# A two-layer decoder trunk in split fp32 on one core: another order for its opening (whole rows of x, products k-tile by k-tile, the first norm from x's rows, low parts shared with GpSimd)

## The reference

```
h = h + 0.5 * RMSNorm_post(SwiGLU(RMSNorm_pre(h)))            # ffn1: d_ff = 2816
h = h + RMSNorm_post(W_out [pool | conv | GLA](RMSNorm_pre(h) @ W_in))
h = h + 0.5 * RMSNorm_post(SwiGLU(RMSNorm_pre(h)))            # ffn2
swiglu(h) = (silu(h @ wg) * (h @ wu)) @ wd
rms_norm(x, g) = x * rsqrt(mean(x*x, -1) + 1e-6) * g
```

## Time and profile before

| | |
|---|---|
| median of 3 runs | 1019.27 us (1018.76, 1019.27, 1021.01) |
| span of the profiled execution | 1017.5 us; the median of the runs is 1.8 us above it, which stands for what lies around the span, as this execution's own time outside the profiler is not listed |
| PE busy | 99% |
| DVE, ACT, POOL busy | 60%, 49%, 25% |
| first matmul on weights | 9.77 us after the span's start |
| first matmul of unit 2 | 25.08 us |

### The profile page before, as it was taken

How to read it: one execution, slowest core, us unless ns; L and a number is a source line. 1 busy time by engine, 2 the same in 40 slices (tenths; PEclk the granted TensorE clock), 3 DMA queues, 4 the chain that set the end, 5 groups by cost and what they waited for, 6 DMA issues and landing times.

```text
span 1017.5 us, 21484 instructions
## 1 busy us (share of the span) xinstructions
PE 1008.4 (99%) x9002; PEld 985.1 (97%) x9002; DVE 614.5 (60%) x610; ACT 498.4 (49%) x565; POOL 256.0 (25%) x179
## 2 busy tenths in 40 slices
PE   8999999999999999999999999999999999999997
PEld 8999999999999999999999999999999999999886
DVE  5744554588968744554477445544889687554452
ACT  5544343566556544443555443435665665434331
POOL 0333330112402333330103333301124014333200
PEclk9999999999999999999999999999999999999999
DMA  9865536635345665435747653357353547666621
GB/s 295 256 202 167 160 114 197 223 125 166 127 141 173 216 192 176 129 114 184 231 131 224 192 166 129 114 194 225 125 167 126 168 149 249 186 191 200 197 73 42
DMA packets 164197, 173.88 MB, mean 171 GB/s; under 512 B 9372, under 2 KB 150936, under 8 KB 164136
## 3 DMA queue, kind: packets, MB, share of 16 engines
q1 hardware_dynamic: 161960, 171.01, 52.9%
q10 hardware_dynamic: 2176, 1.98, 0.8%
HBM read 171.91 MB, written 1.06 MB: 170 GB/s over the span
## 4 chain that ended last, share of the span: by engine, by line
PE 97%; ACT 1%; DMA 1%; DVE 1%; SPq 0%; issue 0%; DVEq 0%
PE ps L1408 25%; PE ps L1410 25%; PE ps L1409 25%; PE ps L1440 2%; PE ps L1425 2%; PE ps L1441 2%; PE ps L1636 2%; PE ps L1635 2%; PE ps L1637 2%; PE ps L1559 2%; PE ps L1600 2%; PE ps L1601 2%; PE ps L1783 1%; DMA raw<-in_ffn_wu 1%; PE ps L1467 1%; ACT w_hi L555 0%
## 5 line engine op out<-in xcount | busy, mean ns | idle before, releaser
L848 DVE TENSOR_TENSOR w_lo<-raw,w_hi 128x2048 fp32r<-128x2048 f32 (+2 forms) x174 | 382.8, 2205 | 278.1 <-ACT w_hi L555 277.7
L1408 PE MATMUL ps<-x_hi,w_hi 128*128 128x272 f32 (+2 forms) x1608 | 462.4, 288 | 0.5 <-DVE w_lo L1026 0.5
L1410 PE MATMUL ps<-x_hi,w_lo 128*128 128x272 f32 (+2 forms) x1608 | 460.3, 286 | 0.0
L1409 PE MATMUL ps<-x_lo,w_hi 128*128 128x272 f32 (+2 forms) x1584 | 453.2, 286 | 0.0
L555 ACT ACTIVATE w_hi<-raw 128x2048 fp32r<-128x2048 f32 (+3 forms) x175 | 312.8, 1791 | 203.1 <-PE ps L1410 142.9
L1408 PEld LDWEIGHTS ps<-x_hi,w_hi 128*128 128x128 f32 x1608 | 302.8, 188 | 2.2 <-DVE w_lo L1026 0.7
L1410 PEld LDWEIGHTS ps<-x_hi,w_lo 128*128 128x128 f32 x1608 | 302.3, 188 | 0.0
L1409 PEld LDWEIGHTS ps<-x_lo,w_hi 128*128 128x128 f32 x1584 | 298.2, 188 | 0.1
L1326 POOL TENSOR_TENSOR up<-gate,up 128x544 f32<-128x544 f32 (+1 forms) x44 | 59.3, 1349 | 314.3 <-ACT gate L663 314.3
L1329 POOL TENSOR_TENSOR hid_lo<-up,hid_hi 128x544 f32 (+3 forms) x44 | 122.0, 2773 | 46.7 <-ACT hid_hi L667 46.7
L663 ACT ACTIVATE gate<-gate 128x544 f32<-128x544 f32 (+1 forms) x44 | 28.7, 653 | 198.9 <-DVE gate L1049 198.9
(11 more groups left out here) (228 smaller groups left out, 1096.0 us busy)
## 6 DMA issues: line engine op xcount, KB each, us to landing
raw<-in_ffn_wg SPq DMA_DIRECT2D x87, 512.0 KB, 4.0
raw<-in_ffn_wu SPq DMA_DIRECT2D x87, 512.0 KB, 5.0
raw<-in_ffn_wd SPq DMA_DIRECT2D x72, 384.0 KB, 3.2
raw<-in_w_in SPq DMA_DIRECT2D x40, 512.0 KB, 4.6
raw<-in_ffn_wd SPq DMA_DIRECT2D x20, 512.0 KB, 4.8
raw<-in_w_out SPq DMA_DIRECT2D x16, 512.0 KB, 4.8
raw<-in_ffn_wd SPq DMA_DIRECT2D x28, 256.0 KB, 3.3
x_tok<-in_x SPq DMA_DIRECT2D x4, 256.0 KB, 5.4
```

Of the source, the lines that this page charges most:

```text
L848: v_.tensor_tensor(w_lo[:, slot, 0:n], raw[:, slot, 0:n], f32(w_hi[:, slot, 0:n]), ALU.subtract)\
L1408: pe.matmul(out_, wh, xh, start=first, stop=False)
L1409: pe.matmul(out_, wh, xl, start=False, stop=False)
L1410: return pe.matmul(out_, wl, xh, start=False, stop=last)
```

## The change

- **Loads.** x comes in two whole row tiles (512 KB each) ahead of SP's weights. The weights of unit 0 come by k-tile: k-tile 0 from ACT's queue, k-tile 1 (`second_in`) and k-tiles 2 and 3 from SP's.
- **PE.** All 16 transposes come first, row tile by row tile, two k-tiles to a bank. The second `stay_warm` goes. The products go k-tile by k-tile, with all three kinds of one k-tile (12 matmuls) before the next. The 64 summing matmuls go.
- **Norm.** ACT squares x's rows (tokens on partitions) with a sum along the row, in three instructions; root and reciprocal act on three columns; three DMAs write the 272 numbers to `r_mem`, one number for each partition and DMA.
- **Low parts.** POOL makes the low part of k-tiles 2 and 3 of unit 1 and of unit 2 (1024 of 2048 floats each); DVE signals `unit_lo` for both once POOL is done.

```diff
 # SP
+                for tt in range(2):
+                    sp.dma_start(x_tok[:, tt, :], x[0, tt * P:(tt + 1) * P, :]).then_inc(x_in[tt], 16)
+                for ks, landed in ((slice(1, 2), second_in), (slice(2, 4), raw_in[0])):
+                    for s_, w in enumerate(weights(phases[0])[0:2]):
+                        sp.dma_start(dst[:, s_, ks], w[:, ks, 0:256]).then_inc(landed, 16)
 # ACT
-            act.dma_start(raw[:, 0, 0:512].rearrange("p (k n) -> p k n", k=2), weights(phases[0])[0][:, 0:2, 0:256])\
-               .then_inc(first_in, 16)
+            for s_, w in enumerate(weights(phases[0])[0:2]):
+                act.dma_start(raw[:, 0, 1024 * s_:1024 * s_ + 256], w[:, 0, 0:256]).then_inc(first_in, 16)
+            def high_part(u, k0, nk, arrived, count, done):
+                act.wait_ge(arrived, count)
+                act.activation(k_part(w_hi, u, k0, nk), k_part(raw, u, k0, nk), ACT.Copy).then_inc(done, 1)
+            def x_squares(n, rows_, src):
+                act.activation(src, src, ACT.Square, accum_out=mean4[0:rows_, n:n + 1]).then_inc(x_sq, 1)
+            high_part(0, 0, 1, first_in, 32, first_hi)
             act.wait_ge(par_ready, 1)
+            act.wait_ge(meta_h, 1)
             high_x(0)
+            high_part(0, 1, 1, second_in, 32, first_hi)
             high_x(1)
+            high_part(0, 2, 2, raw_in[0], 32, unit_hi)
             high_x(2)
             high_x(3)
-            high_unit(1, UNIT)
+            high_part(1, 0, 2, raw_in[1], 32, first_hi)
+            high_x(4)
+            high_x(5)
+            high_part(1, 2, 2, raw_in[1], 32, unit_hi)
+            high_x(6)
+            high_x(7)
             high_unit(2, UNIT)
-            for kk in range(KT):
-                act.activation(f[:, kk, :], h[:, kk, :], ACT.Square).then_inc(sq_ready, 1)
+            for tt in range(2):
+                x_squares(tt, P, x_tok[:, tt, :])
+            x_squares(2, NMETA, meta_tok[:, :])
...
+                    act.wait_ge(x_sq, 3)
+                    act.activation(mean4[:, 0:3], mean4[:, 0:3], ACT.Sqrt, bias=eps[:, :], scale=1.0 / D).then_inc(pre_root, 1)
+                    act.wait_ge(pre_inv, 1)
+                    whole = r_mem[0].rearrange("j t -> (j t)")
+                    for n, (to, rows_) in enumerate(((NMETA, P), (NMETA + P, P), (0, NMETA))):
+                        act.dma_start(whole[to:to + rows_].rearrange("(p a) -> p a", a=1), root4[0:rows_, n:n + 1])                           .then_inc(r_stored, 16)
 # DVE
+            low_part(0, 0, 1, first_hi, 1, first_lo)
+            first_h(0, 1)
+            first_h(1, 1)
+            first_h(2, 2)
+            low_x(0)
+            low_part(0, 1, 1, first_hi, 2, first_lo)
+            low_x(1)
+            first_h(4, 2)
+            low_part(0, 2, 2, unit_hi, 1, unit_lo)
+            low_x(2)
+            low_x(3)
+            first_h(6, 2)
+            low_part(1, 0, 2, first_hi, 3, first_lo)
             for kk in range(4, KT):
                 low_x(kk)
+            v_.wait_ge(first_lo, 3)
+            v_.wait_ge(pool_lo, 1)
+            v_.sem_inc(unit_lo, 1)
+            low_part(2, 0, 2, unit_hi, 3, first_lo)
+            v_.wait_ge(first_lo, 4)
+            v_.wait_ge(pool_lo, 2)
+            v_.sem_inc(unit_lo, 1)
+            v_.wait_ge(pre_root, 1)
+            v_.reciprocal(root4[:, 0:3], mean4[:, 0:3]).then_inc(pre_inv, 1)
 # POOL
+            for u in (1, 2):
+                pool.wait_ge(unit_hi, u + 1)
+                pool.tensor_tensor(k_part(w_lo, u, 2, 2), k_part(raw, u, 2, 2), f32(k_part(w_hi, u, 2, 2)), ALU.subtract)\
+                    .then_inc(pool_lo, 1)
 # PE
+                    for kg in range(KT):
+                        pe.wait_ge(xh_ready, kg + 1)
+                        if highs[kg]:
+                            pe.wait_ge(*highs[kg])
+                        products(w_hi, x_hi, kg)
+                        if lows_[kg]:
+                            pe.wait_ge(*lows_[kg])
+                        products(w_lo, x_hi, kg)
+                        pe.wait_ge(xl_ready, kg + 1)
+                        last = products(w_hi, x_lo, kg)
+                        if kg % 4 == 3:
+                            last.then_inc(unit_used, 1)
-                pe.wait_ge(sq_ready, KT)
-                for kk in range(KT):
-                    last = add_tile(4, f[:, kk], t0, kk == 0, kk == KT - 1)
-                last.then_inc(ss_pre, 1)
-                with_low(1)
-            first_tiles(0)
-            stay_warm(0, 1)
+            for tt in range(2):
+                pe.wait_ge(x_in[tt], 16)
+                for kk in range(KT):
+                    at = 2 * P * (kk % 2) + tt * P
+                    last = pe.transpose(ps[:, 4 + kk // 2, at:at + P], x_tok[:, tt, kk * P:(kk + 1) * P], ident)
+                    if tt:
+                        last.then_inc(ends_tr, 1)
```

More of the change, by code:

```diff
@@ L985, in _, with low_part @@
             v_.sem_inc(up_evac, 1)
[L987 to L996, removed]
+            def low_part(u, k0, nk, highs, count, done):
+                v_.wait_ge(highs, count)
+                v_.tensor_tensor(k_part(w_lo, u, k0, nk), k_part(raw, u, k0, nk), f32(k_part(w_hi, u, k0, nk)),
+                                 ALU.subtract).then_inc(done, 1)
             v_.wait_ge(ends_tr, 1)
@@ L1516, in decay_gate @@
                     last.then_inc(z_mm, 1)
-                def with_low(j):
-                    view = view_of((u0 + j) % RING)
-                    for kk in range(4):
-                        kg = 4 * j + kk
-                        pe.wait_ge(xl_ready, kg + 1)
-                        for mm in range(4):
-                            last = pe.matmul(ps[:, mm, 0:T], view(w_hi, kk, mm), x_lo[:, kg, :],
-                                             start=False, stop=kg == KT - 1)
-                    last.then_inc(unit_used, 1)
                 def sums():
@@ L1562, in first_units, with products @@
                 def first_units():
-                    def products(w, j, k_list):
-                        view = view_of(j)
-                        for kk in k_list:
-                            kg = 4 * j + kk
-                            pe.wait_ge(xh_ready, kg + 1)
-                            for mm in range(4):
-                                pe.matmul(ps[:, mm, 0:T], view(w, kk, mm), x_hi[:, kg, :],
-                                          start=kg == 0 and w is w_hi, stop=False)
+                    def products(w, xs_, kg):
+                        view = view_of(kg // 4)
+                        for mm in range(4):
+                            last = pe.matmul(ps[:, mm, 0:T], view(w, kg % 4, mm), xs_[:, kg, :],
+                                             start=kg == 0 and w is w_hi and xs_ is x_hi, stop=kg == KT - 1 and xs_ is x_lo)
+                        return last
@@ L1573, in first_units @@
+                    highs = ((first_hi, 1), (first_hi, 2), (unit_hi, 1), None, (first_hi, 3), None, (unit_hi, 2), None)
+                    lows_ = ((first_lo, 1), (first_lo, 2), (unit_lo, 1 + RING), None, (first_lo, 3), None, (pool_lo, 1), None)
                     pe.wait_ge(par_ready, 1)
                     pe.wait_ge(meta_h, 1)
-                    pe.wait_ge(first_hi, 2)
-                    products(w_hi, 0, (0, 1))
-                    first_tiles(4)
-                    pe.wait_ge(first_lo, 2)
@@ L1579, in first_units @@
-                    products(w_lo, 0, (0, 1))
-                    pe.wait_ge(unit_hi, 1)
-                    products(w_hi, 0, (2, 3))
-                    pe.wait_ge(unit_lo, 1 + RING)
-                    products(w_lo, 0, (2, 3))
-                    with_low(0)
-                    pe.wait_ge(unit_hi, 2)
-                    products(w_hi, 1, range(4))
-                    pe.wait_ge(unit_lo, 2 + RING)
-                    products(w_lo, 1, range(4))
+                    for kg in range(KT):
[10 more added lines that the diff above has]
+                            last.then_inc(unit_used, 1)
@@ L1678, in _ @@
             last.then_inc(meta_tr, 1)
-            def first_tiles(k0):
-                pe.wait_ge(x_in[k0 // 4], 32)
-                for kk in range(k0, k0 + 4):
-                    if kk >= 4:
-                        pe.wait_ge(h_ready, kk - 3)
-                    for tt in range(2):
-                        last = pe.transpose(ps[:, 4 + kk % 4, tt * P:(tt + 1) * P],
-                                            x_tok[:, tt, kk * P:(kk + 1) * P], ident)
-                    last.then_inc(ends_tr, 1)
-            first_tiles(0)
-            stay_warm(0, 1)
+            for tt in range(2):
[5 more added lines that the diff above has]
+                        last.then_inc(ends_tr, 1)
             for ph in phases:
```

88 lines of the change are left out of this document (29 added, 59 removed).

## The result

The changed kernel takes 1026.19 us (median of 4 runs, 1025.25 to 1027.19), the kernel before 1019.01 us (4 runs, 1018.42 to 1021.01) beside it: a ratio of 1.0073, 95% interval 1.0061 to 1.0085. It is 0.7% slower. Its profiled execution took 1026.33 us with a span of 1024.5 us, 7.0 us more than the 1017.5 of before.

A forecast was written before the change was run, and what follows sets the result against it. PE, busy 99% of the span, was taken to bound the kernel. Unit 2's 0.9 us gain became 0.35 us lost at unit 3; span 1017.85 us, with runs' median 1.8 above the span, gave 1019.6 us, range 1017.2 to 1021.3.

The forecast's parts named there:

- The start: Opening: x's second half lands at 9.0 us, then transposes, copy and `high_x`; first product at 10.65 us.
- x arrives faster: Rival, opening: 4 KB pieces bring landings 0.9 us earlier; 2.2 us off, 1017.0 us; chance 0.12.
- POOL's low parts: Units 1 and 2: POOL and DVE take turns, 2.3 us per half; PE waits 0.8; unit 2 starts at 24.15.
- POOL gets in first: Rival: x late, POOL's halves precede `low_x` 4 and 5; unit 2 at 26.4; 1.4 to 1.9 us slower, 1020.9; chance 0.18.
- Unit 3: Three store issues take 2.4 us, delaying unit 3's low part; PE waits 1.3, starting 0.35 us later than before; chance 0.45.
- The norm comes late: Rival at unit 4: stores landing s after last issue delay PE beyond s = 4.3 us; 2.5 us, 1022.1; chance 0.05.
- a sign of being wrong: After unit 3: the prediction is wrong if PE is ever short of weights or banks there.
- The range: Whole kernel: 1017.2 to 1021.3 us, to leave out no more than 0.2; chances 0.17 faster, 0.14 slower, 0.69 within.
- The ceiling: Unit 2: PE fed without a stop from 10.65 us would reach it at 22.7, 2.4 us earlier than before.

The follow-up runs named there:

- the probe: The kernel spreading roots by PE, plus three unneeded stores of 272 4-byte numbers side by side; POOL's instruction behind them started 9.5 us after the last issue.

## Why the prediction was wrong

The prediction was 1019.6 us, range 1017.2 to 1021.3; the median was 1026.19. By its own steps:

**The start** was right in its number, 10.61 against 10.65 us, by luck. x's rows landed 3.7 and 5.3 us after their issues at 1.2 and 1.7, 7.0 at the latest instead of the 9.0 taken, since the rate from 4 to 5 us was 405 GB/s where it had been 253. This is the mechanism of the rival "x arrives faster". The Trainium skill (Perfetto Trace Analysis, "DMA Optimizations") holds that going from 2 KB to 4 KB pieces can raise throughput, and these rates agree, 405 against 253 GB/s; that the pieces alone did it, no run separates. But x did not decide when the products start. DVE's list has the low part of k-tile 0's weights ahead of its first copy to `h`, and these weights had just landed at 8.03:

```profile
8.03 0.63 ACT L614 ACTIVATE w_hi<-raw 128x512 fp32r<-128x512 f32 x1 [3.81 <-DMA raw<-in_ffn_wu]
8.69 0.69 DVE L1004 TENSOR_TENSOR w_lo<-raw,w_hi 128x512 fp32r<-128x512 f32 x1 [1.93 <-ACT w_hi L614]
9.30 1.34 DVE L1014 COPY h<-ps 128x256 f32<-128x256 f32 x3
9.83 0.52 ACT L610 ACTIVATE x_hi<-h,par 128x272 fp32r<-128x272 f32 x1 [1.17 <-DVE h L1014]
```

The sixteen transposes took 3.65 us, at the pace that the first eight of before had the earlier trace rows. They did not decide either: in the kernel without POOL's low parts they took 1.97 us and ended at 7.9, and the first product still came at 10.21. With two copies to `h` put ahead of that low part (the new order) it came at 9.27.

**POOL's low parts** were right in kind: POOL and DVE took turns.

```profile
15.87 5.29 POOL L1335 TENSOR_TENSOR w_lo<-raw,w_hi 128x1024 fp32r<-128x1024 f32 x2 [14.18 <-ACT w_hi L614]
```

```profile
15.15 1.21 DVE L1004 TENSOR_TENSOR w_lo<-raw,w_hi 128x1024 fp32r<-128x1024 f32 x1
16.28 6.00 DVE L1019 SCALAR_TENSOR_TENSOR x_lo<-h,par,x_hi 128x272 fp32r<-128x272 f32 x4
22.20 1.21 DVE L1004 TENSOR_TENSOR w_lo<-raw,w_hi 128x1024 fp32r<-128x1024 f32 x1
...
27.24 2.29 DVE L862 TENSOR_TENSOR w_lo<-raw,w_hi 128x2048 fp32r<-128x2048 f32 x1 [3.47 <-ACT w_hi L558]
```

POOL's two halves read 2.7 and 2.6 us (2.3 of work was taken), and four `low_x` last 6.0 us together, two of them some 2.6 each, where four took 1.73. The order was not the one taken: POOL began at 15.87, before `low_x` 4 could at 16.28. That is "POOL gets in first", brought about by ACT being early and not by x being late. PE waited 1.9 us in two places instead of 0.8, and unit 2 started at 25.11 instead of 24.15. That step was 1.0 us off; it was inside the rival's 26.4.

**Unit 3** was wrong in size and harmless. The three issues took 1.39 us, 0.46 each, not 2.4. The low part was ready at 29.5 and PE came at 31.1: no wait, where 0.35 us of delay was the prediction's net effect.

**The norm comes late** is the step that failed. The prediction named the mechanism, the place (banks 0 to 3 at unit 4), the point from which it decides, a landing s of 4.3 us, and a sign of being wrong that came true: PE short of banks after unit 3. Its sum left this wait at nothing, because it judged s by the wrong row: the row store, 0.6 us after its issue, is four pieces of 272 B; the new ones are 272 pieces of 4 B side by side. The trace of before has no store of single numbers, so nothing held s under 4.3 us, and yet the case got a chance of only 0.05 and a price of 2.5 us. Measured: s = 9.6 us. The rival's own chain then gives the wait: last issue done 25.2, landing 9.6, spreading load 5.7, evacuation 1.4 make 41.9, and PE came at 37.15: 4.8 us. The row-store run shows it directly: with stores in rows s is 2.5 us, and 6 us are back.

**The clock** stood nowhere in the sum. It added 2.5 us of slower products to a start of unit 4 that was 4.9 us late, and in the profiled execution of the kernel without stores 1.5 us to a wait of 2.3.

**The range** left out more than its own chances allow. They put 0.17 below 1017.2 us and 0.14 above 1021.3, 0.31 together and not 0.2, and count "x faster" as wholly under 1017.2 in one place and as half of it in another.

**The ceiling** of 22.7 us at unit 2 could be reached: with the roots spread on the core, no POOL and h copied first, unit 2 starts there, at 22.73, and what the prediction expected to be given back at unit 3 is kept: in that trace the first mixing stage's products start at 242.9 us instead of 245.4.

## What to carry to other kernels

Before a reduction's results are stored straight from a column, one number per partition, count on 9 to 11 us until they have landed if they lie side by side in memory, and on other loads that take 7 to 12 us instead of 4 to 7 meanwhile; if they are only wanted on the same core, spread them there (here by small matmuls of 0.9 us and one copy of 0.4). Where a trace has no row for an operation's shape, the nearest row is a bound and not a value: work out the landing from which it decides, and ask what holds the landing below that. And price a wait of PE of 2.3 us or more together with the slower products that may follow it.

## What the runs showed of the hardware

- 272 numbers of 4 B stored side by side in DRAM by three DMAs landed 9.4, 9.6 and 10.9 us after the end of the last issue in three kernels, and 9.5 us in the probe; 512 B apart 4.7 us, as 64 B pieces 4.4 us. Weights' loads of 512 KB issued just ahead of them or while they were under way landed after 7.0 to 12.5 us in the kernels read above, where the corresponding loads took 4.0 to 5.0 us beside row stores and 3.8 to 6.6 us beside none.
- The granted clock fell to 0.50 (1.2 GHz) in PE's waits of 4.7 us (the changed kernel) and 6.9 us (without POOL's low parts), and the next products cost 0.227 us each instead of 0.125 in the changed kernel. After a wait of 2.3 or 2.4 us ahead of the first product it fell in the profiled executions of two kernels of five (the one that spreads by PE, and the probe with its pieces side by side), and stayed at 1.00 in three; after 1.1 and 1.4 us it stayed. So such a wait is worth its own length or 1.5 us more, and which of the two isn't told by its length.
- The sixteen transposes took 3.65 us in the changed kernel, where they began at 6.36, and 1.97 in the kernel without POOL's low parts, where they began at 5.94, with the same work ahead of them; the windows read 1.00 in both. The two kernels are the same up to there, so this differs from one execution to the next. It costs little here, because faster transposes only lengthen the wait behind them.
- A square with a row sum on ACT took 1.04 to 1.06 us for 1024 floats plus a read of 0.18 to 0.19: close to the prediction's lower bound of 1.06, a copy of as many floats.
